# One core: an attention stage gives up the expert slots hidden in it, and the merge stage after it works all 128, sixteen to a tile

## The chip, the cores and the metric

The kernel runs on one core of one Trainium2 chip. The metric is the device time of one execution in microseconds. The compute engines named below are TensorE (PE; its weight loads are PEld), VectorE (DVE), ScalarE (ACT) and GpSimd (POOL); SyncE (SP) issues most transfers, and POOL issues the indirect ones, called gathers here.

## The reference, cut to what matters

Two groups of tokens, a sample of 256 and a prompt of 1024, pass through the same layer with the same weights: a mixer (a windowed attention A, a dense attention B, and a gated merge of the two), then a retrieval from 16384 experts, then a norm.

```python
def parallel_mixer(h, ...):
    ...
    oa = window_attention(...)
    ob = dense_attention(...)
    gates = sigmoid(h @ w_gate + b_gate); ga, gb = split(gates)
    merged = ga * (oa @ w_oa) + gb * (ob @ w_ob)
    return merged @ w_out

def peer(h, ...):                      # T tokens, 8 heads x 16 experts = 128 slots for each
    ...
    u, v = expert_u[idx], expert_v[idx]
    act = gelu(einsum('chkd,cd->chk', u, xc))
    return einsum('chk,chkd->cd', g * act, v)
```

For each token 128 experts are chosen. A slot is one expert for each of the 128 tokens of a tile: its rows (u and v, 2048 numbers for each token) are fetched from HBM, u is dotted with the token, the dot goes through gelu and is multiplied by the gate g, and v times that weight is added to a sum.

## The kernel before, in words

The program goes through stages with a barrier behind each (`build`): the sample's projection, attention, merge and choice of experts; then the prompt's projection, attention and merge, and last the prompt's experts. A stage works on tiles of 128 tokens, of which the sample has two and the prompt eight.

The choice of experts for the sample writes h, the indices and the gates g of both tiles to HBM, without fetching an expert. The fetching and summing for these two tiles is spread over the prompt's stages, beside their own work. Sample tile 0 runs in the prompt's projection (class `Background`). Sample tile 1 runs in the prompt's attention and merge (class `Hidden`, made by `Hiding(sample, 1)` in `build`). That second tile is what the change is about. Its parts are:

- `Hidden.load`: SP fetches h, the indices and g (line 260).
- `Hidden.gather_upto`: POOL issues one gather for a slot (line 283), 128 rows of 8 KB, into one of five ring places. From the sixth slot on it first waits until the slot five before it has been added.
- `Hidden.dot_of`: DVE multiplies u with h and sums (line 296); this waits for the gather to land.
- `Hidden.gelu`: ACT (line 334).
- `Hidden.add_of`: DVE forms the weight (line 305) and adds v times the weight to the sum (line 313). This frees the ring place.

In the attention stage (`phase_attend`) eight slots are worked in each of the eight prompt tiles, so 64 in all. A tile has eight steps g, one for each head of B and two of A, and `hide(i, 2g)` and `hide(i, 2g + 1)` place one dot or one add of the hidden tile into DVE's order, before and behind `max_b`. POOL computes the rotary embedding of the next tile and then issues the gathers. ACT evaluates four gelus at a time, at g = 1 and 5. When there is a hidden tile, two details differ: `Fills` gives all copies of transposed A probabilities (`pT_a`) to ACT, and ACT runs `exp_a` ahead of them. Without one, as in the sample's attention, ACT and DVE take one copy each and `exp_a` comes behind it.

In the merge stage (`phase_merge`) PE multiplies the mixed rows with `w_oa` and `w_ob` (four groups for a tile, line 1408), transposes the merged rows (line 1420), and multiplies with `w_out` (line 1431). DVE multiplies PE's results with the gates (`part`, line 1377, four for a tile), adds the two branches (`merged`, line 1383, two), and adds x (`xt`, line 1391, one). POOL adds the bias to the gates of a tile (`add_bias`, line 1322), and ACT takes the sigmoid (line 1350) and copies the transposed rows (line 1357). The function `turns` sets the order of the tiles: the branches of tile i are begun before the projection of tile i-1 is finished. The hidden work is spread by `Plan`: 2 x (128 - `first`) operations, one dot and one add for a slot, cut evenly over 48 places, of which a tile has six (two ahead of each half's products, as `hide(i, 0)` to `hide(i, 3)`, and two ahead of the `xt` of the tile before). With `first` = 64 a place holds 2 or 3 operations. `Plan.pool` lets POOL issue gathers up to five slots beyond what will have been added at that place, and POOL's order is written out: `add_bias(0)`, places 0 and 1, `add_bias(1)`, then in each tile three places, `add_bias(i + 1)`, three places.

`Early` fetches the first half of `w_oa` in the attention stage so that the merge has it at its start.

## Time and profile before

| what | value |
|---|---|
| median of the two runs | 4945.34 us (4940.06 to 4950.62) |
| the profiled execution's own time | 4939.81 us |
| its span, first to last instruction | 4937.9 us |
| busy in the span | PE 63%, DVE 68%, ACT 21%, POOL 35% |
| mean granted TensorE clock | 0.739 of full speed |
| moved by DMA | 1568.77 MB, mean 318 GB/s |

Times in the rows are microseconds from the start of the span unless marked ns. A row of the timeline gives the start, the duration, the engine, the line in the kernel, the operation with what it writes and reads, and in brackets how long the engine sat idle before it and who released it. A row that groups instructions gives the count, the busy time, the mean duration in ns and, behind the bar, the idle time of the engine in front of them. A row of the table by stretches gives the length of the stretch, then for each engine its busy time and number of instructions, then the granted clock, the share of the DMA engines' time that was used, and the rate.

### The profile page before, as it was taken

To read this page: it belongs to the slowest core of one execution; us is meant where nothing else is said; L and a number is where in the kernel's file an instruction comes from. 1 tells how busy PE (TensorE), PEld (TensorE's weight loads), DVE (VectorE), ACT (ScalarE), POOL (GpSimd) and SP (SyncE) were. 2 spreads that over 40 slices of the span, in tenths; PEclk is the share of its full clock that TensorE was granted. 3 is DMA by queue.
4 is the path that set the end of the run, shared out by engine and by line. 5 is a ranking of instruction groups with operands and counts; after the bars stand their busy time and mean duration, and the time that the engine had idled before them with its cause. 6 is when DMAs were issued, how large, how long until landed. Compare 5 with 4: busy or idle time off the path is not lost.

```text
span 4937.9 us, 72225 instructions
## 1 busy us (share of the span) xinstructions
PE 3098.5 (63%) x27052; PEld 1782.3 (36%) x27052; DVE 3340.8 (68%) x7744; ACT 1042.4 (21%) x2853; POOL 1728.8 (35%) x1393
## 2 busy tenths in 40 slices
PE   7686389885999989955545455445455444454433
PEld 6545367663777744432212112122122122121000
DVE  4426777786888866658867767667667577677554
ACT  3311111221555521111121121111211211211111
POOL 0200033323344323224444444444444444444443
PEclk9897699987999999966656666666566566565555
DMA  6143288897445477689999999999999999999998
GB/s 238 62 165 113 95 325 330 330 341 283 165 150 190 156 310 280 245 315 385 389 401 393 393 404 394 389 404 403 406 389 389 402 392 392 394 391 383 407 392 326
DMA packets 281852, 1568.77 MB, mean 318 GB/s; under 512 B 28064, under 2 KB 48032, under 8 KB 112928
## 3 DMA queue, kind: packets, MB, share of 16 engines
q0 software_dynamic: 184320, 1342.26, 68.9%
q1 hardware_dynamic: 97184, 221.90, 12.1%
q8 instruction: 215, 3.52, 0.3%
q14 instruction: 133, 1.09, 0.1%
HBM read 1510.52 MB, written 53.53 MB: 317 GB/s over the span
## 4 chain that ended last, share of the span: by engine, by line
DMA 32%; issue 7%; PE 7%; DVE 5%; POOL 4%; ACT 2%; another core or an unknown queue 0%; POOLq 0%; DVEq 0%; SPq 0%; ACTq 0%
DMA prompt_exp_ring<-in_experts_dram,prompt_exp_idx 29%; PE prompt_exp_acc L1966 6%; POOL prompt_exp_ring L1619 4%; DVE prompt_exp_junk L1864 3%; DMA prompt_exp_ring<-in_experts_dram,prompt_exp_idx_all 3%; ACT prompt_exp_diag L1696 2%; PE prompt_exp_qp L1927 1%; DVE prompt_exp_pos L1743 0%; DVE prompt_exp_best L1739 0%; PE prompt_exp_qp L1987 0%; DVE prompt_exp_dot L1864 0%; DMA prompt_exp_wq<-in_w_query_dram 0%; DVE prompt_exp_crest L1748 0%; DVE prompt_exp_topi L1743 0%
## 5 line engine op out<-in xcount | busy, mean ns | idle before, releaser
L1966 PE MATMUL prompt_exp_acc<-prompt_exp_ring,prompt_exp_diag 32*32 32x512 f32 x16384 | 936.3, 940 | 1396.1 <-ACT prompt_exp_diag L1696 1395.3
L1864 DVE CUSTOM_DVE_ANT_0 prompt_exp_junk<-prompt_exp_ring,prompt_exp_h_now 128x1024 bf16<-128x1024 f32 x1024 | 1244.9, 1227 | 698.3 <-DMA prompt_exp_ring<-in_experts_dram,prompt_exp_idx 654.0
L1619 POOL DMA_INDIRECT prompt_exp_ring<-in_experts_dram,prompt_exp_idx x896 | 1032.0, 1152 | 1369.8 <-PE prompt_exp_acc L1966 1205.3
L1966 PEld LDWEIGHTS prompt_exp_acc<-prompt_exp_ring,prompt_exp_diag 32*32 32x32 f32 x16384 | 168.6, 127 | 1948.6 <-issue 1945.9
L1690 ACT ACTIVATE prompt_exp_ge<-prompt_exp_dot 128x2 f32<-128x2 f32 x512 | 104.1, 203 | 2286.8 <-DVE prompt_exp_dot L1864 2286.6
L144 POOL DMA_INDIRECT bg_ring<-in_experts_dram,bg_idx x128 | 175.1, 1368 | 667.2 <-DVE bg_acc L180 367.3
L1927 PEld LDWEIGHTS prompt_exp_qp<-prompt_exp_hT,prompt_exp_wq 128*128 128x128 f32 x2048 | 314.6, 243 | 144.7 <-issue 141.8
L1927 PE MATMUL prompt_exp_qp<-prompt_exp_hT,prompt_exp_wq 128*128 128x128 f32 x2048 | 338.1, 334 | 4.2 <-DMA prompt_exp_wq<-in_w_query_dram 2.4
L283 POOL DMA_INDIRECT sample_hid_ring<-in_experts_dram,sample_hid_idx x128 | 131.8, 1030 | 512.7 <-DVE sample_hid_acc L313 496.0
L703 PE MATMUL prompt_proj_acc<-prompt_proj_w_hi,prompt_proj_hT_hi 128*128 128x512 f32 x640 | 261.1, 408 | 27.0 <-ACT prompt_proj_w_hi L596 23.1
L1696 ACT ACTIVATE prompt_exp_diag<-prompt_exp_fold,prompt_exp_wgt 128x32 f32<-128x32 f32 x1024 | 264.4, 306 | 0.4 <-issue 0.2
L704 PE MATMUL prompt_proj_acc<-prompt_proj_w_hi,prompt_proj_hT_lo 128*128 128x512 f32 x640 | 258.7, 404 | 0.0
L1619 POOL DMA_INDIRECT prompt_exp_ring<-in_experts_dram,prompt_exp_idx_all x128 | 150.7, 1178 | 267.7 <-PE prompt_exp_acc L1966 154.6
L169 DVE CUSTOM_DVE_ANT_0 bg_junk<-bg_ring,bg_h 128x1024 bf16<-128x1024 f32 x128 | 154.2, 1222 | 98.3 <-DMA bg_ring<-in_experts_dram,bg_idx 97.6
L296 DVE CUSTOM_DVE_ANT_0 sample_hid_junk<-sample_hid_ring,sample_hid_h 128x1024 bf16<-128x1024 f32 x128 | 202.1, 1579 | 20.3 <-DMA sample_hid_ring<-in_experts_dram,sample_hid_idx 10.8
L718 PE MATMUL prompt_proj_acc<-prompt_proj_w_lo,prompt_proj_hT_hi 128*128 128x512 f32 x640 | 172.0, 418 | 53.5 <-DVE prompt_proj_w_lo L639 53.5
L180 DVE SCALAR_TENSOR_TENSOR bg_acc<-bg_ring,bg_w,bg_acc 128x1024 f32<-128x1024 f32 x128 | 164.4, 1285 | 4.6
L313 DVE SCALAR_TENSOR_TENSOR sample_hid_acc<-sample_hid_ring,sample_hid_w,sample_hid_acc 128x1024 f32<-128x1024 f32 x127 | 163.0, 1283 | 2.9
L718 PEld LDWEIGHTS prompt_proj_acc<-prompt_proj_w_lo,prompt_proj_hT_hi 128*128 128x128 f32 x640 | 127.9, 202 | 88.6 <-DVE prompt_proj_w_lo L639 57.4
L1858 DVE TENSOR_TENSOR prompt_exp_wgt<-prompt_exp_ge,prompt_exp_g_now 128x2 f32<-128x2 f32 x512 | 83.0, 162 | 109.7 <-ACT prompt_exp_ge L1690 101.6
L703 PEld LDWEIGHTS prompt_proj_acc<-prompt_proj_w_hi,prompt_proj_hT_hi 128*128 128x128 f32 x640 | 124.2, 194 | 60.3 <-ACT prompt_proj_w_hi L596 25.6
L704 PEld LDWEIGHTS prompt_proj_acc<-prompt_proj_w_hi,prompt_proj_hT_lo 128*128 128x128 f32 x640 | 124.2, 194 | 29.9
(349 smaller groups left out, 5046.0 us busy)
## 6 DMA issues: line engine op xcount, KB each, us to landing
sample_proj_w<-in_w_all_dram SPq DMA_DIRECT2D x10, 2048.0 KB, 9.5
prompt_proj_w<-in_w_all_dram SPq DMA_DIRECT2D x10, 2048.0 KB
proj_dram<-prompt_proj_stage SPq DMA_DIRECT2D x80, 256.0 KB
prompt_exp_ring<-in_experts_dram,prompt_exp_idx POOLq DMA_INDIRECT x896
sample_exp_wq<-in_w_query_dram SPq DMA_DIRECT2D x4, 2048.0 KB, 15.5
prompt_att_q<-proj_dram SPq DMA_DIRECT2D x16, 512.0 KB
mixed_dram<-prompt_att_OT SPq DMA_DIRECT2D x8, 1024.0 KB, 3.8
prompt_mrg_mixT<-mixed_dram SPq DMA_DIRECT2D x8, 1024.0 KB
```

What stands on the lines that cost most here:

```text
L144: self.nc.gpsimd.indirect_dma_start(out=self.ring[:, k % self.RING, :], out_offset=None, in_=self.experts, in_offset=bass.IndirectOffsetOn ...
L180: last = nc.vector.scalar_tensor_tensor(self.acc[:], self.ring[:, (k + c) % self.RING, D:], self.w[:, c:c + 1], self.acc[:], ALU.mult, ALU ...
L296: self.nc.vector.tensor_tensor_reduce(out=self.junk[:], in0=self.ring[:, s % self.RING, 0:D], in1=self.h[:], scale=1.0, scalar=0.0, op0=AL ...
L313: nc.vector.scalar_tensor_tensor(self.acc[:], v, w, self.acc[:], ALU.mult, ALU.add).then_inc(self.added, 1)
L703: nc.tensor.matmul(acc[:, u % 4, :], hT_hi[:, k, cols], hi[:, k, :], start=(first and k == 0), stop=False)
L704: ins = nc.tensor.matmul(acc[:, u % 4, :], hT_lo[:, k, cols], hi[:, k, :], start=False, stop=(last and k == KD - 1))
L718: ins = nc.tensor.matmul(acc[:, u % 4, :], hT_hi[:, k, cols], lo[:, k, :], start=(first and k == 0), stop=(last and k == KD - 1))
L1619: nc.gpsimd.indirect_dma_start(out=ring[:, s % RING, :], out_offset=None, in_=experts, in_offset=bass.IndirectOffsetOnAxis(ap=column(s), a ...
L1696: last = nc.scalar.activation(diag[:, (g - 1) % 2, c, :], fold[:], ACT.Copy, scale=wgt[:, s:s + 1])
L1864: nc.vector.tensor_tensor_reduce(out=junk[:, s % 2, :], in0=ring[:, s % RING, 0:D], in1=h_now[:], scale=1.0, scalar=0.0, op0=ALU.mult, op1 ...
L1927: last = nc.tensor.matmul(qp[:, h % 2, p * P:(p + 1) * P], wq[:, k, (2 * h + p) * P:(2 * h + p + 1) * P], hT[:, k * P:(k + 1) * P], start= ...
L1966: last = nc.tensor.matmul(acc[at:at + Q, rows, :], diag[k, (g - 1) % 2, c, :], ring[k, s % RING, D + half * 512:D + half * 512 + 512], sta ...
```

## The change

`attend` for the prompt gets no hidden tile, and `merge` starts it at slot 0 instead of slot 64. The hidden tile's h, indices and gates are therefore loaded at the start of the merge, behind the first mixed rows and ahead of the weights.

```diff
@@ phase_merge, block.sync @@
                 load_mix(0)
                 if not bg:
                     early.load(sp)
+                elif first == 0:
+                    bg.load(sp)
                 for h in range(2):
@@ build @@
             early = Early(nc, Mem(nc, front, sems, "early"), w_oa)
-            attend(prompt, hidden, 0, early)
-            merge(prompt, hidden, SLOTS // 2, early)
+            attend(prompt, None, 0, early)
+            merge(prompt, hidden, 0, early)
         release(nc, sems)
```

The changed kernel's lines behind 1282 have numbers that are two higher. `Plan` now has 256 operations for the same 48 places, 5 or 6 in each. Three places of the program show what that does.

DVE in the merge, from the `xt` of one tile (line 1391, 1393 in the changed kernel) to the first `part` of the tile after the next (line 1377, 1379). Before:

```order
L1391 TENSOR_TENSOR prompt_mrg_xt<-prompt_mrg_Z,prompt_mrg_xt 128x1024
L305 TENSOR_TENSOR sample_hid_w<-sample_hid_ge,sample_hid_g 128x1
L313 SCALAR_TENSOR_TENSOR sample_hid_acc<-sample_hid_ring,sample_hid_w,sample_hid_acc 128x1024
L296 ISA sample_hid_junk,sample_hid_dot<-sample_hid_ring,sample_hid_h 128x1024
L296 ISA sample_hid_dot 128x1
L305 TENSOR_TENSOR sample_hid_w<-sample_hid_ge,sample_hid_g 128x1
L313 SCALAR_TENSOR_TENSOR sample_hid_acc<-sample_hid_ring,sample_hid_w,sample_hid_acc 128x1024
L1377 TENSOR_TENSOR prompt_mrg_part<-prompt_mrg_Y,prompt_mrg_gate 128x512
```

The same stretch in the changed kernel:

```order
L1393 TENSOR_TENSOR prompt_mrg_xt<-prompt_mrg_Z,prompt_mrg_xt 128x1024
L296 ISA sample_hid_junk,sample_hid_dot<-sample_hid_ring,sample_hid_h 128x1024
L296 ISA sample_hid_dot 128x1
L305 TENSOR_TENSOR sample_hid_w<-sample_hid_ge,sample_hid_g 128x1
L313 SCALAR_TENSOR_TENSOR sample_hid_acc<-sample_hid_ring,sample_hid_w,sample_hid_acc 128x1024
L296 ISA sample_hid_junk,sample_hid_dot<-sample_hid_ring,sample_hid_h 128x1024
L296 ISA sample_hid_dot 128x1
L305 TENSOR_TENSOR sample_hid_w<-sample_hid_ge,sample_hid_g 128x1
L313 SCALAR_TENSOR_TENSOR sample_hid_acc<-sample_hid_ring,sample_hid_w,sample_hid_acc 128x1024
L296 ISA sample_hid_junk,sample_hid_dot<-sample_hid_ring,sample_hid_h 128x1024
L296 ISA sample_hid_dot 128x1
L1379 TENSOR_TENSOR prompt_mrg_part<-prompt_mrg_Y,prompt_mrg_gate 128x512
```

A place held three hidden operations here (add, dot, add) and now holds five (dot, add, dot, add, dot).

POOL at the start of the merge. Before, with the gathers of the last attention tile in the first row (16 of them: eight of that tile and eight that go with the tile before):

```order
L283 DMA sample_hid_ring<-in_experts_dram,sample_hid_idx 128x2048 x16
L1322 TENSOR_TENSOR prompt_mrg_gate<-prompt_mrg_gate,prompt_mrg_bias 128x2048
L283 DMA sample_hid_ring<-in_experts_dram,sample_hid_idx 128x2048 x2
L1322 TENSOR_TENSOR prompt_mrg_gate<-prompt_mrg_gate,prompt_mrg_bias 128x2048
L283 DMA sample_hid_ring<-in_experts_dram,sample_hid_idx 128x2048 x6
L1322 TENSOR_TENSOR prompt_mrg_gate<-prompt_mrg_gate,prompt_mrg_bias 128x2048
L283 DMA sample_hid_ring<-in_experts_dram,sample_hid_idx 128x2048 x8
```

And in the changed kernel:

```order
L283 DMA sample_hid_ring<-in_experts_dram,sample_hid_idx 128x2048 x5
L1324 TENSOR_TENSOR prompt_mrg_gate<-prompt_mrg_gate,prompt_mrg_bias 128x2048
L283 DMA sample_hid_ring<-in_experts_dram,sample_hid_idx 128x2048 x4
L1324 TENSOR_TENSOR prompt_mrg_gate<-prompt_mrg_gate,prompt_mrg_bias 128x2048
L283 DMA sample_hid_ring<-in_experts_dram,sample_hid_idx 128x2048 x14
L1324 TENSOR_TENSOR prompt_mrg_gate<-prompt_mrg_gate,prompt_mrg_bias 128x2048
L283 DMA sample_hid_ring<-in_experts_dram,sample_hid_idx 128x2048 x16
```

The ring's first five gathers now stand in the merge ahead of the first `add_bias`, and nine of the 128 stand ahead of the second one, where 71 did.

ACT in the attention, one step with a transposed query (`qT`) between two others. Before:

```order
L1000 ACTIVATE prompt_att_prob_b,prompt_att_rsum<-prompt_att_Sb,prompt_att_nm 128x1024
L908 COPY prompt_att_qT<-prompt_att_tb 128x512
L334 ACT_TABLE_LOAD
L334 ACTIVATE sample_hid_ge<-sample_hid_dot 128x4
L908 COPY prompt_att_pT_b<-prompt_att_tb 128x512
L994 ACT_TABLE_LOAD
L994 ACTIVATE prompt_att_prob_a,prompt_att_rsum<-prompt_att_Sm,prompt_att_nm 128x385 x2
L908 COPY prompt_att_pT_a<-prompt_att_tb 128x384 x2
```

And in the changed kernel:

```order
L1000 ACTIVATE prompt_att_prob_b,prompt_att_rsum<-prompt_att_Sb,prompt_att_nm 128x1024
L908 COPY prompt_att_qT<-prompt_att_tb 128x512
L908 COPY prompt_att_pT_b<-prompt_att_tb 128x512
L908 COPY prompt_att_pT_a<-prompt_att_tb 128x384
L994 ACTIVATE prompt_att_prob_a,prompt_att_rsum<-prompt_att_Sm,prompt_att_nm 128x385 x2
```

The gelu and two loads of a function table are gone from ACT; it copies one `pT_a` of a step instead of two (DVE does the other) and computes the exponentials of A behind it.

## Rows read from the trace of the kernel before

**Rows 1.** The page, the chain that ended last, by line.

```profile
DMA prompt_exp_ring<-in_experts_dram,prompt_exp_idx 29%; PE prompt_exp_acc L1966 6%; POOL prompt_exp_ring L1619 4%; DVE prompt_exp_junk L1864 3%; DMA prompt_exp_ring<-in_experts_dram,prompt_exp_idx_all 3%; ACT prompt_exp_diag L1696 2%; PE prompt_exp_qp L1927 1%; DVE prompt_exp_pos L1743 0%; DVE prompt_exp_best L1739 0%; PE prompt_exp_qp L1987 0%; DVE prompt_exp_dot L1864 0%; DMA prompt_exp_wq<-in_w_query_dram 0%; DVE prompt_exp_crest L1748 0%; DVE prompt_exp_topi L1743 0%
```

**Rows 2.** Stretches: the attention's tiles, the merge's start, one merge tile.

```profile
1262.00:1757.00 495.00, 462.08 (x3182) 358.58 (x3179) 428.18 (x922) 284.93 (x602) 190.04 (x120) 1.00 0.44 162
1757.00:1800.00 43.00, 32.44 (x69) 14.23 (x70) 15.89 (x23) 5.38 (x8) 9.01 (x4) 0.81 0.92 361
1966.80:2008.80 42.00, 42.00 (x105) 19.07 (x104) 26.66 (x39) 7.11 (x12) 13.25 (x9) 1.00 0.72 275
```

**Rows 3.** Timeline of DVE in the merge, late.

```profile
1954.41 1.22 DVE L296 CUSTOM_DVE_ANT_0 sample_hid_junk<-sample_hid_ring,sample_hid_h 128x1024 bf16<-128x1024 f32 x1
...
1956.95 1.22 DVE L296 CUSTOM_DVE_ANT_0 sample_hid_junk<-sample_hid_ring,sample_hid_h 128x1024 bf16<-128x1024 f32 x1
...
1966.76 1.23 DVE L1391 TENSOR_TENSOR prompt_mrg_xt<-prompt_mrg_Z,prompt_mrg_xt 128x1024 f32<-128x1024 f32 x1 [6.04 <-PE prompt_mrg_Z L1431]
...
2008.84 1.23 DVE L1391 TENSOR_TENSOR prompt_mrg_xt<-prompt_mrg_Z,prompt_mrg_xt 128x1024 f32<-128x1024 f32 x1 [6.05 <-PE prompt_mrg_Z L1431]
```

**Rows 4.** Groups of DVE in the merge, 1757 to 2110.

```profile
L1377 DVE TENSOR_TENSOR prompt_mrg_part<-prompt_mrg_Y,prompt_mrg_gate 128x512 f32<-128x512 f32 x32 | 22.1, 690 | 71.2 <-PE prompt_mrg_Y L1408 52.2 <-ACT prompt_mrg_gate L1350 19.1
L1383 DVE TENSOR_TENSOR prompt_mrg_merged<-prompt_mrg_part 128x512 f32<-128x512 f32 x16 | 14.7, 917 | 1.9 <-PE prompt_mrg_tb L1420 1.5
```

**Rows 5.** Timeline of POOL and DVE, one of two `add_bias` and its neighbour.

```profile
1863.28 5.11 POOL L1322 TENSOR_TENSOR prompt_mrg_gate<-prompt_mrg_gate,prompt_mrg_bias 128x2048 f32<-128x2048 f32 x1 [3.98 <-DMA prompt_mrg_gate<-proj_dram]
1863.94 5.53 DVE L296 CUSTOM_DVE_ANT_0 sample_hid_junk<-sample_hid_ring,sample_hid_h 128x1024 bf16<-128x1024 f32 x1
...
1985.55 4.52 POOL L1322 TENSOR_TENSOR prompt_mrg_gate<-prompt_mrg_gate,prompt_mrg_bias 128x2048 f32<-128x2048 f32 x1
...
1988.78 1.31 DVE L305 TENSOR_TENSOR sample_hid_w<-sample_hid_ge,sample_hid_g 128x1 f32<-128x1 f32 x1
```

**Rows 6.** Timeline of SP, PE, POOL and DVE, the merge's start.

```profile
1762.75 0.32 SPq L1272 DMA_DIRECT2D prompt_mrg_mixT<-mixed_dram  x1
1767.56 10.19 PE L1408 MATMUL prompt_mrg_Y<-early_w,prompt_mrg_mixT 128*128 128x512 f32 x16 [14.61 <-DMA prompt_mrg_mixT<-mixed_dram]
1777.99 4.50 POOL L1322 TENSOR_TENSOR prompt_mrg_gate<-prompt_mrg_gate,prompt_mrg_bias 128x2048 f32<-128x2048 f32 x1 [26.62 <-DMA prompt_mrg_bias<-in_b_gate_dram]
1784.46 0.69 DVE L1377 TENSOR_TENSOR prompt_mrg_part<-prompt_mrg_Y,prompt_mrg_gate 128x512 f32<-128x512 f32 x1 [19.05 <-ACT prompt_mrg_gate L1350]
1797.96 4.50 POOL L1322 TENSOR_TENSOR prompt_mrg_gate<-prompt_mrg_gate,prompt_mrg_bias 128x2048 f32<-128x2048 f32 x1 [5.82 <-DMA prompt_mrg_gate<-proj_dram]
```

**Rows 7.** The tile `prompt_mrg_xt`: its DVE instructions, first and last start.

```profile
L1391 DVE TENSOR_TENSOR prompt_mrg_xt<-prompt_mrg_Z,prompt_mrg_xt x8: 1224/1224/1226, 1840.5 to 2109.0; 128x1024 f32<-128x1024 f32 x8
```

**Rows 8.** The tile `sample_hid_ring`: landing of gathers, issued 1800 to 1850, then to 2093.

```profile
DMA to landing us min/median/max: 8.2/12.3/16.5
...
DMA to landing us min/median/max: 5.6/6.1/11.3
```

**Rows 9.** Stretch in the prompt's experts.

```profile
3000.00:4000.00 1000.00, 491.28 (x6852) 200.88 (x6852) 685.40 (x1773) 155.71 (x624) 431.95 (x376) 0.63 0.99 397
```

**Rows 10.** DMA queues in the merge, 1757 to 2110: packets, MB, share.

```profile
q0 software_dynamic: 8517, 61.96, 45.7%
q1 hardware_dynamic: 9338, 38.29, 27.6%
```

**Rows 11.** Waits of PE in the attention, 1262 to 1757: us, times, longest.

```profile
PE prompt_att_tb L1134 <- ACT prompt_att_prob_b L1000: 11.8, 12, 1.1
PE prompt_att_Op L1194 <- ACT prompt_att_pT_a L908: 9.7, 14, 0.7
PE prompt_att_tb L1134 <- ACT prompt_att_OT L908: 5.0, 6, 0.8
```

**Rows 12.** Timeline of DVE and PE, the attention's first tile.

```profile
1221.04 6.00 DVE L296 CUSTOM_DVE_ANT_0 sample_hid_junk<-sample_hid_ring,sample_hid_h 128x1024 bf16<-128x1024 f32 x1 [2.62 <-DMA sample_hid_ring<-in_experts_dram,sample_hid_idx]
1229.67 1.97 PE L1134 MATMUL prompt_att_tb<-prompt_att_ident,prompt_att_prob_b 128*128 128x128 f32 x8 [5.70 <-ACT prompt_att_prob_b L1000]
```

## The prediction

> **What bounds the kernel now.** I read the chain that ended last, then the table by stretches, then the timeline of each engine in the merge. The chain is mostly the gathers of the prompt's experts [rows 1]. That stage comes behind a barrier, holds none of the changed work, and should keep its length. So the question is the length of two stages ahead of it.
>
> In the attention's tiles PE is busy 462 of 495 us, DVE 428 [rows 2]. The end is PE's, with some waits. The last merge tiles are PE alone: 42.0 of 42.0 us, DVE only 26.7 [rows 2], and DVE sits 6 us in front of `xt` waiting for PE [rows 3]. Two `xt` are 42.08 us apart [rows 3]: that is a merge tile now. The merge runs from SP's first load at 1762.75 [rows 6], which I call M, to the last `xt`, which starts at 2109.0 and takes 1.2 [rows 7]: M + 347.5.
>
> **What the attention gains.** It loses 64 slots, that is 64 dots, 64 adds, 16 weight products, 16 gelus with two table loads each, the loads of h, indices and gates, and 69 gathers. What of that is on PE's path is what PE waited for. Between 1262 and 1757 it waited 11.8 us for `prob_b` and 5.0 us for the copy of `OT` [rows 11]. Both come late because hidden dots stand in front of `max_b` on DVE, so I count both as gone: 17. The 9.7 us put down to `pT_a` [rows 11] fall where PE waits for DVE's division, in front of which nothing hidden stands; they stay. In the first tile one hidden dot takes 6.00 us and PE then waits 5.70 [rows 12], its next matmuls running slower; I take 8 for this. One `pT_a` copy of a step moves to DVE, behind `max_b`: DVE has lost two hidden operations of about 1.2 us in that step, and PE has 16 products of B in between, so it costs nothing. ACT now has `exp_a` behind that copy; losing one copy covers it. If that cover failed it would be some 0.5 us for each of 64 steps, 32. I take -25, with bounds -36 (all waits gone) and +7 (cover failed).
>
> **What the merge's DVE must do.** Two dots with one weight product and one add between them start 1954.41 and 1956.95, so a slot costs 2.54 [rows 3]. Sixteen are 40.6. The tile's own products by mean duration are 4 x 0.69 + 2 x 0.92 [rows 4] + 1.2 for `xt` [rows 7] = 5.8. Consecutive operations overlap by some 7% (a slot's durations add up to more than its spacing), so 5.4. Together 46.0 against PE's 42.08. DVE takes PE's place as the bound, even if nothing else happens.
>
> Something else does: `add_bias`. POOL's operation ran 1863.28 to 1868.39, and a dot that DVE started at 1863.94 took 5.53 instead of 1.22; in a later tile the one-column weight product, started inside POOL's 4.52 us, ended when POOL did [rows 5]. (The Trainium skill, GPSIMD Engine Reference, Specifications, says that POOL's SBUF interfaces are shared with VectorE, with contention for instructions with two SBUF inputs. Dot, weight product and add are such; by this rule every `add_bias` stops DVE's now unbroken row of them, by its absence a tile would be 46.) Now DVE was mostly waiting for PE meanwhile; with DVE busy throughout, each costs up to 4.5. A tile: 50.5.
>
> **What the DMA must do.** Experts are fetched at 376 gathers in 1000 us with the engines at 0.99 [rows 9]: 2.66 for a slot of 1.05 MB. Sixteen are 42.6; a tile also moves 3.15 MB (mixed rows, gates, x in, x2 out), 7.7 at about 410 GB/s: 50.3. DVE and DMA would both be nearly full, with a ring of five between them. A gather in the loaded part of the merge takes 12.3 us to land, in the unloaded part 6.1 [rows 8]. A ring place is held for the wake and issue on POOL (0.8), the landing, and two dots and two adds with weights (5.1): five slots in 12.0 or 18.2 us, 2.4 or 3.6 for one. The tile allows 50.5/16 = 3.15. So it is sometimes short. Also, while `add_bias` runs, POOL issues nothing and the DMA engines run dry. I take 53.5 for the first six tiles and 51 for the last two, which load no more mixed rows or gates: mean 53. The bounds are 46.0 (no stop, no wait) and 16 x 3.6 = 58.
>
> **The start of the merge.** Before, the ring was full and DVE's first `part` started at M + 21.7, behind a bias that landed at M + 15.2; the second `add_bias` had its gates at M + 35.2 [rows 6]. Now h (0.6 MB with indices and gates) goes ahead of the weights, and POOL issues five gathers (5.2 MB) before its first `add_bias`. At the 361 to 410 GB/s seen [rows 2], with the two queues sharing, the bias lands near M + 24 and the first `part` starts at about M + 30. Only nine gathers stand ahead of the second `add_bias`. Its gates lie behind 12 MB of direct loads, and 9.4 MB of gathers join them: M + 54. DVE uses up its nine slots by about M + 49 and waits: `add_bias` to M + 58.5, issue, a landing of 8 to 10: M + 68. By then 17 of the 256 hidden operations are done.
>
> **The sum.** 239 operations are left, 32 to a tile: 7.47 tiles x 53 = 396. M + 68 + 396 = M + 464; the last projection on PE is longer than the two places beside it by some 3, and `xt` is 1.2: M + 468. Against M + 347.5 that is +120. With the attention's -25: +95. The profiled execution is 4939.8, its span 1.9 less; that gives 5035. The median shown is 5.5 above it, so I say 5038.
>
> **Rivals.**
> (a) The stops of `add_bias` fall mostly into waits that exist anyway and the ring keeps up: a tile is 47 to 48. 68 + 7.47 x 47.5 + 4 = 427: +79 - 25 = +54, 4997. For it: DVE paid only about 1.2 for such a stop late in the merge [rows 5]. Against it: then DVE was idle half of the time.
> (b) The ring decides: 58 for a tile. 68 + 433 + 4 = 505: +158 - 25 = +133, 5075. For it: the landing of 12.3 when loaded [rows 8]. Against it: DMA is at 0.72 in a present tile [rows 2] and a landing there is 6.1.
> (c) HBM limits lower, at the 361 GB/s of the merge's start [rows 2] for as long as both queues are full. Then 38.3 MB [rows 10] and 134 MB of gathers take 477, the end is M + 485: +138 - 25 = +113, 5056. Against it: the experts run at 397 [rows 9] for a thousand microseconds. (The Trainium skill, DMA: Bandwidth & Descriptors, Where 436 GB/s comes from, names about 358 GB/s as what binds between HBM and SBUF on a core, and by it the merge would take 481; the trace's 397 disagrees.)
> (d) Not slower: DVE takes the eight further slots into its waits. It decides if a tile's DVE work stays below 46 with the start as before. Then M + 21.7 + 7.85 x 46 + 4 = M + 387: +39, and with the attention's full -36 it is +3, 4945; with a `part` that overlaps better, some us below before. For it: DVE idles 15.4 of 42 [rows 2]. Against it: eight slots are 20.3, more than 15.4, and the ring is empty at the start.
> (e) That the change does less than it says can't be: the orders show all 128 slots in the merge.
>
> **How the numbers follow.** Forecast 0.52, own range 5010 to 5065. (a) 0.21, (b) 0.19, (c) 0.03, (d) 0.05. The range 4980 to 5085 leaves out most of (d) and the far end of (b). Slower by over 2%, which is about what a measurement of this kernel can tell from no change, begins at 5044: all of (b) and (c) and two fifths of the forecast, 0.43. Within 2%: 0.56. Faster by over 2%: 0.01, since not even all of the attention's waits together with the smallest merge give 99 us.
>
> **What would show it.** Right: attention tiles some 2 us shorter (the `OT` stores closer together), no PE wait for `prob_b` of more than a few us in sum; in the merge two `xt` 50 to 56 us apart, PE with idle time in front of the branches waiting for DVE's `part`, DVE over 85% busy, a dot or weight product of some 5 us beside nearly every `add_bias`; a first `part` near M + 30; a DVE wait for a gather of over 10 us near M + 50; DMA share above 0.9. Wrong: `xt` 42 us apart with DVE waiting for PE (then (d)), or over 57 with DVE waiting for the ring after most slots (then (b)), or an attention that isn't shorter.

## The result and the profile after

The changed kernel takes 5046.3 us (two runs, 5039.9 and 5052.8) against 4945.3 of the kernel before: ratio 1.0208, interval 1.0189 to 1.0228. It is slower by 101 us, and the interval lies on both sides of 2%. The forecast was 5038, its own range 5010 to 5065.

The page of the changed kernel, its span, busy times, DMA and chain:

```profile
span 5038.0 us, 72280 instructions
PE 3111.4 (62%) x27052; PEld 1781.5 (35%) x27052; DVE 3348.6 (66%) x7856; ACT 980.5 (19%) x2805; POOL 1742.5 (35%) x1393
...
DMA packets 281852, 1568.77 MB, mean 311 GB/s; under 512 B 28064, under 2 KB 48032, under 8 KB 112928
...
DMA 31%; issue 7%; PE 7%; DVE 6%; POOL 4%; ACT 2%; POOLq 0%; DVEq 0%; SPq 0%; ACTq 0%
```

The chain still ends in the experts' gathers, as in [rows 1]. It does not tell where 100 us came from: followed back, it begins at 2217.4 us, with the first loads of the experts' stage, and the two stages that changed lie ahead of the barrier before that. So they are measured by their marks: SP's first load of each and the last `xt`.

| | before | after |
|---|---|---|
| attention, first load to the merge's first load (M) | 573.9 | 542.7 |
| M in the trace | 1762.75 | 1728.70 |
| first `xt` | M + 77.8 | M + 129.1 |
| end of the last `xt` | M + 347.5 | M + 477.6 |
| one full merge tile | 42.08 | 55.96 |
| from there to the end of the span | 2827.7 | 2831.7 |

Attention -31.2, merge +130.1, an attention that starts 2.8 earlier, 4.0 behind the merge: +100 of span. The last two are within what the other runs show: the attention starts between 1186.0 and 1193.4 in them, and for the stage behind the merge see below.

**The attention.** The stretch of its tiles and the groups of PE in it (busy, mean ns | idle before, releaser), changed kernel:

```profile
core 0: us, PE busy (x) PEld busy (x) DVE busy (x) ACT busy (x) POOL busy (x), PEclk, DMA share, GB/s
1262.00:1720.00 458.00, 447.93 (x3103) 350.28 (x3103) 271.30 (x769) 210.19 (x485) 111.75 (x60) 1.00 0.11 38
```

```profile
L1194 PE MATMUL prompt_att_Op<-prompt_att_vB,prompt_att_pT_b 128*128 128x128 f32 x928 | 114.1, 276 | 9.7 <-DVE prompt_att_O L1061 9.7
...
L1134 PE MATMUL prompt_att_tb<-prompt_att_ident,prompt_att_prob_b 128*128 128x128 f32 x464 | 63.3, 279 | 0.0
```

These answer to [rows 2] and [rows 11]: the waits for `prob_b` and `OT` are gone, and the 9.7 that [rows 11] puts down to `pT_a` stay, now named `prompt_att_O`, which is DVE's division.

**The merge's start.** POOL and DVE, changed kernel (start, us, ... [idle before <-releaser]); this answers to [rows 6]:

```profile
1750.44 4.49 POOL L1324 TENSOR_TENSOR prompt_mrg_gate<-prompt_mrg_gate,prompt_mrg_bias 128x2048 f32<-128x2048 f32 x1 [8.31 <-DMA prompt_mrg_bias<-in_b_gate_dram]
...
1785.61 4.51 POOL L1324 TENSOR_TENSOR prompt_mrg_gate<-prompt_mrg_gate,prompt_mrg_bias 128x2048 f32<-128x2048 f32 x1 [16.29 <-DMA prompt_mrg_gate<-proj_dram]
```

```profile
1746.18 1.23 DVE L296 CUSTOM_DVE_ANT_0 sample_hid_junk<-sample_hid_ring,sample_hid_h 128x1024 bf16<-128x1024 f32 x1 [17.35 <-DMA sample_hid_ring<-in_experts_dram,sample_hid_idx]
1750.92 5.10 DVE L296 CUSTOM_DVE_ANT_0 sample_hid_junk<-sample_hid_ring,sample_hid_h 128x1024 bf16<-128x1024 f32 x1 [3.50 <-DMA sample_hid_ring<-in_experts_dram,sample_hid_idx]
...
1799.99 1.22 DVE L296 CUSTOM_DVE_ANT_0 sample_hid_junk<-sample_hid_ring,sample_hid_h 128x1024 bf16<-128x1024 f32 x1 [16.79 <-DMA sample_hid_ring<-in_experts_dram,sample_hid_idx]
```

With an empty ring DVE's first dot waits 17.4 us. Behind the second `add_bias`, which waits 16.3 for tile 1's gates with the gathers queued behind it, DVE waits 16.8, and dots again at M + 71.3.

**A merge tile.** The last `xt` group, then stretches: a long one, and two microseconds at a time around one `add_bias`, which POOL ran 2002.42 to 2007.35 with a dot of 5.53 us beside it:

```profile
L1393 DVE TENSOR_TENSOR prompt_mrg_xt<-prompt_mrg_Z,prompt_mrg_xt x8: 1216/1217/1225, 1857.8 to 2205.1; 128x1024 f32<-128x1024 f32 x8
```

```profile
core 0: us, PE busy (x) PEld busy (x) DVE busy (x) ACT busy (x) POOL busy (x), PEclk, DMA share, GB/s
1860.00:2080.00 220.00, 175.53 (x411) 78.15 (x410) 196.15 (x282) 31.09 (x77) 99.23 (x67) 0.89 0.91 356
...
1992.00:1996.00 4.00, 4.00 (x6) 1.44 (x6) 2.59 (x4) 0.20 (x1) 2.28 (x2) 0.51 1.01 426
...
2004.00:2006.00 2.00, 2.00 (x6) 0.90 (x5) 2.00 (x1) 0.00 (x0) 2.00 (x1) 1.00 0.96 397
2006.00:2008.00 2.00, 2.00 (x6) 0.81 (x5) 2.00 (x1) 0.00 (x0) 1.85 (x2) 1.00 0.16 66
2008.00:2010.00 2.00, 2.00 (x6) 0.95 (x5) 1.97 (x5) 0.20 (x1) 1.26 (x1) 1.00 0.08 12
2010.00:2012.00 2.00, 2.00 (x6) 0.89 (x5) 1.97 (x4) 0.20 (x1) 1.14 (x1) 1.00 0.93 279
```

Groups of DVE and PE from 1860 to 2080, and below them the same stretch in the kernel before:

```profile
L296 DVE CUSTOM_DVE_ANT_0 sample_hid_junk<-sample_hid_ring,sample_hid_h 128x1024 bf16<-128x1024 f32 x64 | 95.4, 1490 | 21.1 <-DMA sample_hid_ring<-in_experts_dram,sample_hid_idx 20.9
L1379 DVE TENSOR_TENSOR prompt_mrg_part<-prompt_mrg_Y,prompt_mrg_gate 128x512 f32<-128x512 f32 x16 | 11.0, 686 | 0.0
...
L1433 PE MATMUL prompt_mrg_Z<-prompt_mrg_wo,prompt_mrg_mT 128*128 128x512 f32 x128 | 65.0, 673 | 44.5 <-ACT prompt_mrg_mT L1359 44.5
```

```profile
1860.00:2080.00 220.00, 220.00 (x544) 99.67 (x543) 141.91 (x204) 35.76 (x61) 69.97 (x47) 1.00 0.70 266
```

Read them together. DVE is busy 196.2 of 220, that is 49.9 of a tile of 55.96, and waits for nothing of PE (0.0 before `part`); it waits 20.9 us for gathered rows, 5.3 a tile. PE, which had 220 busy of 220, now waits 44.5 for `mT`, a copy of what DVE merged. The two engines have changed roles. And the stop does two things at once: DVE stands still, so it frees no place, and POOL issues nothing, so the queued gathers land and the DMA engines fall from 397 to 66 and 12 GB/s.

**Where in the tile the rows come late.** One tile of the changed kernel in order of time, up to 1920: SP's three loads for the next tile, every wait of DVE for a row, and `add_bias`:

```profile
1866.28 0.33 SPq L1278 DMA_DIRECT2D prompt_mrg_xt<-in_x_dram  x1
1866.66 0.57 SPq L1272 DMA_DIRECT2D prompt_mrg_mixT<-mixed_dram  x1
1867.28 0.46 SPq L1275 DMA_DIRECT2D prompt_mrg_gate<-proj_dram  x1
1870.81 1.22 DVE L296 CUSTOM_DVE_ANT_0 sample_hid_junk<-sample_hid_ring,sample_hid_h 128x1024 bf16<-128x1024 f32 x1 [1.03 <-DMA sample_hid_ring<-in_experts_dram,sample_hid_idx]
1874.37 1.23 DVE L296 CUSTOM_DVE_ANT_0 sample_hid_junk<-sample_hid_ring,sample_hid_h 128x1024 bf16<-128x1024 f32 x1 [0.93 <-DMA sample_hid_ring<-in_experts_dram,sample_hid_idx]
1879.19 1.23 DVE L296 CUSTOM_DVE_ANT_0 sample_hid_junk<-sample_hid_ring,sample_hid_h 128x1024 bf16<-128x1024 f32 x1 [0.74 <-DMA sample_hid_ring<-in_experts_dram,sample_hid_idx]
1884.15 1.23 DVE L296 CUSTOM_DVE_ANT_0 sample_hid_junk<-sample_hid_ring,sample_hid_h 128x1024 bf16<-128x1024 f32 x1 [2.34 <-DMA sample_hid_ring<-in_experts_dram,sample_hid_idx]
1889.35 4.93 POOL L1324 TENSOR_TENSOR prompt_mrg_gate<-prompt_mrg_gate,prompt_mrg_bias 128x2048 f32<-128x2048 f32 x1
1917.99 1.23 DVE L296 CUSTOM_DVE_ANT_0 sample_hid_junk<-sample_hid_ring,sample_hid_h 128x1024 bf16<-128x1024 f32 x1 [0.68 <-DMA sample_hid_ring<-in_experts_dram,sample_hid_idx]
```

The other three tiles of the stretch look alike: 18.8 of the 20.9 us lie within 20 us behind SP's loads of the next tile's x, mixed rows and gates, and none within 16 us behind an `add_bias`. Gathers issued between 1870 and 1880 took a median of 12.6 us to land, those between 1894 and 1914, behind the addition, 6.7. So it is the tile loads that make rows late. The dry time behind the stop, when DVE stands still as well, does not.

### The profile page after: what moved, and what is told of

Same layout as the page of the kernel before. It is cut to its first block, busy times and chain, and to the rows that moved or that the text cites. A ratio compares the mean times of both kernels' runs of the same rounds, so it can differ in the third digit from the quotient of the medians.

```text
span 5038.0 us, 72280 instructions
## 1 busy us (share of the span) xinstructions
PE 3111.4 (62%) x27052; PEld 1781.5 (35%) x27052; DVE 3348.6 (66%) x7856; ACT 980.5 (19%) x2805; POOL 1742.5 (35%) x1393
## 4 chain that ended last, share of the span: by engine, by line
DMA 31%; issue 7%; PE 7%; DVE 6%; POOL 4%; ACT 2%; POOLq 0%; DVEq 0%; SPq 0%; ACTq 0%
DMA prompt_exp_ring<-in_experts_dram,prompt_exp_idx 28%; PE prompt_exp_acc L1968 6%; POOL prompt_exp_ring L1621 4%; DVE prompt_exp_junk L1866 3%; DMA prompt_exp_ring<-in_experts_dram,prompt_exp_idx_all 3%; ACT prompt_exp_diag L1698 2%; PE prompt_exp_qp L1929 1%; DVE prompt_exp_pos L1745 0%; DVE prompt_exp_best L1741 0%; DVE prompt_exp_dot L1866 0%; DMA prompt_exp_wq<-in_w_query_dram 0%; DVE prompt_exp_hit L1788 0%; DVE prompt_exp_hit L1782 0%; DVE prompt_exp_crest L1750 0%; DVE prompt_exp_sel L1792 0%
## 5 line engine op out<-in xcount | busy, mean ns | idle before, releaser
L144 POOL DMA_INDIRECT bg_ring<-in_experts_dram,bg_idx x128 | 178.3, 1393 | 660.0 <-DVE bg_acc L180 360.4
L283 POOL DMA_INDIRECT sample_hid_ring<-in_experts_dram,sample_hid_idx x128 | 156.8, 1225 | 364.3 <-DVE sample_hid_acc L313 223.8
L296 DVE CUSTOM_DVE_ANT_0 sample_hid_junk<-sample_hid_ring,sample_hid_h 128x1024 bf16<-128x1024 f32 x128 | 186.0, 1453 | 74.2 <-DMA sample_hid_ring<-in_experts_dram,sample_hid_idx 74.0
L1433 PE MATMUL prompt_mrg_Z<-prompt_mrg_wo,prompt_mrg_mT 128*128 128x512 f32 x256 | 127.0, 659 | 82.5 <-ACT prompt_mrg_mT L1359 67.6
L718 PEld LDWEIGHTS prompt_proj_acc<-prompt_proj_w_lo,prompt_proj_hT_hi 128*128 128x128 f32 x640 | 130.1, 205 | 86.0 <-DVE prompt_proj_w_lo L639 54.2
## 6 DMA issues: line engine op xcount, KB each, us to landing
sample_exp_wq<-in_w_query_dram SPq DMA_DIRECT2D x4, 2048.0 KB, 18.2
```

The lines of the kernel that those rows point to most:

```text
L144: self.nc.gpsimd.indirect_dma_start(out=self.ring[:, k % self.RING, :], out_offset=None, in_=self.experts, in_offset=bass.IndirectOffsetOn ...
L296: self.nc.vector.tensor_tensor_reduce(out=self.junk[:], in0=self.ring[:, s % self.RING, 0:D], in1=self.h[:], scale=1.0, scalar=0.0, op0=AL ...
L718: ins = nc.tensor.matmul(acc[:, u % 4, :], hT_hi[:, k, cols], lo[:, k, :], start=(first and k == 0), stop=(last and k == KD - 1))
```

## Experiments

My theory for the tile was a sum: DVE's work 45.9, the stop 4.3, rows that come late 5 to 6. The rivals: DMA is the floor and everything on DVE is only its shadow; or PE's chain holds all. Repeats set the scale: 19 runs of the kernel before, taken together, lay between 4935.6 and 4957.9, two single ones beside other experiments came to 4954.2 and 4930.3, and the stage behind the merge took 2812 to 2838 in the runs of the table, though nothing in it differs. A single total says little below 20 us, so what follows rests on marks inside each trace: "tile" is a fifth of the time from the first `xt` to the sixth, "end" the end of the last `xt` after M. The total is that of the traced execution, for e11 and e12 the median of ten (their traced ones took 4942.6 and 4952.9).

| run | tile | first `xt` | end | total |
|---|---|---|---|---|
| before | 42.08 | M + 77.8 | M + 347.5 | 4939.8 |
| changed | 55.96 | M + 129.1 | M + 477.6 | 5039.9 |
| e1 half the slots | 42.09 | M + 96.0 | M + 365.7 | 4924.9 |
| e2 no bias addition | 51.89 | M + 124.6 | M + 454.1 | 5000.9 |
| e3 half the rows | 52.20 | M + 120.9 | M + 446.3 | 5005.8 |
| e4 no sum | 51.99 | M + 123.6 | M + 447.0 | 4999.6 |
| e5 half the rows, no bias | 47.87 | M + 111.6 | M + 415.7 | 4975.5 |
| e6 bias on VectorE | 53.93 | M + 127.0 | M + 466.9 | 5032.9 |
| e7 ring filled early | 56.25 | M + 114.9 | M + 464.9 | 5013.1 |
| e8 second bias late | 55.85 | M + 126.1 | M + 474.4 | 5032.7 |
| e9 ring of seven | 50.31 | M + 125.0 | M + 442.0 | 5010.2 |
| e10 no sum, no bias | 48.82 | M + 121.5 | M + 430.3 | 4988.3 |
| e11 four a tile, 96 in the merge | 45.21 | M + 96.3 | M + 378.9 | 4948.3 |
| e12 the same, bias on VectorE | 45.82 | M + 94.7 | M + 379.2 | 4945.2 |

**e1: the attention's gain and the start alone.**

```diff
-        plan = Plan(first, SLOTS - first, PLACES * G, 1, 1)
+        plan = Plan(first, SLOTS // 2 if bg else SLOTS, PLACES * G, 1, 1)
```

> The changed kernel with only 64 of the second sample tile's 128 slots worked at all, eight to a tile of the merge, none in the attention; the other 64 are left out of the computation. It holds the attention's gain and the merge's new start alone. My theory (the loss is the 16 slots a tile, the start adds some 20 us): attention 542.7 us as in the changed kernel (573.9 before), tiles of the merge back at TensorE's 42.1 us, merge end at M+365 to M+375 (M+347.5 before), total about 4933 us. Rival (the start alone costs most of the +130, by the weights that come late): merge end beyond M+420, total above 4985. Rival (the attention's gain is given back behind it): attention again near 570.

The attention took 542.4 again, the tile fell back to 42.09, the end came at M + 365.7. In the groups of the trace DVE waits for PE again before `xt`:

```profile
L1393 DVE TENSOR_TENSOR prompt_mrg_xt<-prompt_mrg_Z,prompt_mrg_xt x8: 1223/1225/1226, 1831.0 to 2099.4; 128x1024 f32<-128x1024 f32 x8
its engine sat idle before it (us, times) until:
  PE prompt_mrg_Z L1433: 45.3, 8
```

So the new start, with an empty ring and the loads of h ahead of the weights, costs 18.2 of the 130; the attention's gain is real and is not given back; the other 112 are the eight further slots to a tile.

**e2 to e5: take a load off each side.** e2 leaves out `add_bias` on POOL, e3 every second gather, e4 the sum, e5 is e2 and e3 in one.

```diff
 def add_bias(i):
     pool.wait_ge(gate_ld[i % 2], 16 * (i // 2 + 1))
+    if bg:
+        pool.sem_inc(biased, 1)
+        return
...
-            nc.vector.scalar_tensor_tensor(self.acc[:], v, w, self.acc[:], ALU.mult, ALU.add)
+            nc.vector.tensor_scalar(self.acc[:, 0:1], v[:, 0:1], w, None, ALU.mult)
...
+            if not (s < self.RING or s % 2 == 0):
+                continue
             self.nc.gpsimd.indirect_dma_start(
```

> The changed kernel, the prompt's merge without GpSimd's addition of the gates' bias; the bias is left out of the computation there. A: VectorE's stop of 4.3 us beside that addition is a real term of the tile and the waits for gathers (5.0) stay: tiles of 51 to 52 us instead of 56.0, merge end near M+448, total near 5015. B: DMA decides and the stop only overlaps with it, the time comes back as waits for gathers: tiles of 55 to 56, total 5035 to 5046.

> The changed kernel with every second gather of an expert row left out after the first five slots; VectorE works all 128 slots with the same instructions, every second one on the row that lies in the ring already. A and B: the waits for gathers (5.0 us a tile) go, VectorE's 45.9 and its stop of 4.3 stay: tiles of 50.2 us, merge end near M+440, total near 5008. Rival (waits for gathers hide a VectorE that would be late anyway, by PE or ACT): tiles stay above 54. Also asked: does the start (first dot at M+17.5, VectorE out of work from M+53 to M+71) get shorter, as DMA is less full? If it is the ring of five slots behind the second bias addition's gate load, the stop stays about 16 us.

> The changed kernel where each slot's addition (1024 columns into the sum) is cut to a product of one column; the sum over the slots is left out. VectorE's work a tile falls from 45.9 to about 31 us, all gathers stay. A (the tile is VectorE's work plus stops plus late rows, and DMA has room): tiles fall to TensorE's 42 to 45 us, total near 4965. B (DMA is a floor by itself: 19.9 MB a tile at 397 GB/s are 50.3 us): tiles of 50 to 52 us, merge end near M+435, total near 5005.

> The changed kernel with both edits of the earlier runs: every second gather left out after the first five slots, and the bias addition of the prompt's merge left out of the computation. Alone, they brought the tile from 56.0 to 52.2 and 51.9 us. Theory D (two near floors: VectorE with its work of 45.9 and the stop of 4.3, and DMA with 19.9 MB at 392 GB/s, 50.8, and 4 to 5 us in which it runs dry behind the stop): with both the tile is VectorE's work alone, 46 to 47 us, merge end near M+415, total near 4975. Rival (something common to all three, TensorE's lowered clock or the chain Y, gate, merged, transpose, Z, holds the tile at 52): tiles of 51 to 52, total above 4998.

The stretch 1860 to 2080 of e2 (columns as in the stretches above):

```profile
1860.00:2080.00 220.00, 185.97 (x443) 82.78 (x441) 193.38 (x301) 35.46 (x86) 83.70 (x69) 0.94 0.98 387
```

The dots' group of e2 in it:

```profile
L296 DVE CUSTOM_DVE_ANT_0 sample_hid_junk<-sample_hid_ring,sample_hid_h 128x1024 bf16<-128x1024 f32 x68 | 83.0, 1221 | 23.7 <-DMA sample_hid_ring<-in_experts_dram,sample_hid_idx 23.4
```

The same stretch of e3, and then its dots:

```profile
1860.00:2080.00 220.00, 181.52 (x425) 80.58 (x423) 207.08 (x301) 35.71 (x85) 59.84 (x38) 0.92 0.62 230
```

```profile
L301 DVE CUSTOM_DVE_ANT_0 sample_hid_junk<-sample_hid_ring,sample_hid_h 128x1024 bf16<-128x1024 f32 x68 | 100.1, 1473 | 10.0 <-DMA sample_hid_ring<-in_experts_dram,sample_hid_idx 10.0
```

The same stretch of e4, and then its dots:

```profile
1860.00:2080.00 220.00, 186.89 (x440) 82.87 (x438) 141.71 (x302) 35.78 (x86) 85.23 (x73) 0.94 0.95 385
```

```profile
L296 DVE CUSTOM_DVE_ANT_0 sample_hid_junk<-sample_hid_ring,sample_hid_h 128x1024 bf16<-128x1024 f32 x69 | 103.3, 1496 | 76.0 <-DMA sample_hid_ring<-in_experts_dram,sample_hid_idx 75.9 <-issue 0.2
```

e2: the dots fell from 1490 ns to 1221, so the stop sat in them and comes from POOL's addition; the tile fell by 4.1, about the stop. The waits for rows stayed at 5.5 a tile (23.4 in 220 us of 51.9 each). Case A held for the tile; the end came 6 us later than I had put it. e3: DVE busy 49.1 of 52.2, waits for rows down to 2.4 a tile, DMA at 0.62. Its tile is 2 above what was expected, since those waits did not vanish. e4: DVE is busy 33.5 of the tile instead of 49.9, and the tile fell by only 4.0, with dots waiting 18 us a tile for rows. That is case B: with DVE this light, DMA decides. DVE's load and DMA's are both near the tile, and neither is a shadow of the other. e5, with both loads lower, came to 47.87 and M + 415.7 where 46 to 47 and M + 415 stood: the rival of something common at 52 is out.

The start in e3: DVE still waited 17.3 us for its first row, but behind the second `add_bias` only 8.0 instead of 16.8. With half the gathers gone, tile 1's gates landed 5 us earlier after M (that `add_bias` started at M + 52.0 for M + 56.9). My expectation there, 16 us, missed.

**e10: DMA alone.** e4 with e2's edit.

> The changed kernel without the sum over the slots (one column instead of 1024) and without the prompt's bias addition, both left out of the computation; all gathers and loads stay. VectorE's work is some 31 us a tile and GpSimd only issues gathers, so what is left is DMA alone beside TensorE's 42.1. If the 52.0 us of the run without the additions were 19.9 MB at the 420 GB/s of its undisturbed stretches plus 4 us dry behind the stop: tiles of 47.5 to 49. If DMA alone takes 50.8 (392 GB/s): tiles of 50 to 51. If DMA is no floor below this: 42.1 to 45.

```profile
1860.00:2080.00 220.00, 199.02 (x469) 88.48 (x468) 130.04 (x317) 36.82 (x88) 71.26 (x71) 0.95 1.01 410
```

Here the DMA engines are full throughout, at 410 GB/s, and a tile of 19.9 MB took 48.82: DMA's own floor. e4 took 3.2 more with the same gathers; that is what the dry time behind a stop costs DMA.

**e9: a deeper ring.**

```diff
-    RING = 5
+    RING = 7
...
-        wo = m.sb("wo", [P, KD, D])
+        wo = m.sb("wo", [P, KD, 512 if bg else D])
```

> The changed kernel with a ring of seven gathered rows instead of five. To make room, only the first half of w_out is held in the merge and used for both halves of Z (the second half of w_out is left out of the computation; TensorE does the same work), and the ring is allocated after the attention. E: the some 5 us a tile by which the tile of 56.0 exceeds each engine's own sum (VectorE 50.2, DMA 50.8) come from a ring too short to bridge the stop and the tile loads, where two near floors alternate: tiles of 51 to 53 us. Rival (DMA's dry time behind the stop is lost whatever the depth, and tile loads take their share): tiles stay at 55 to 56.

```profile
1860.00:2080.00 220.00, 188.81 (x437) 83.74 (x436) 215.89 (x313) 36.72 (x87) 102.73 (x75) 0.92 0.99 398
```

```profile
L296 DVE CUSTOM_DVE_ANT_0 sample_hid_junk<-sample_hid_ring,sample_hid_h 128x1024 bf16<-128x1024 f32 x71 | 90.5, 1274 | 1.0 <-DMA sample_hid_ring<-in_experts_dram,sample_hid_idx 1.0
```

This settles the 5.3 us. With two more places the waits for rows fell from 20.9 to 1.0 in 220 us, DVE was busy 98%, and the tile was 50.31: DVE's sum of 50.2 and nothing else. `add_bias` still ran on POOL and still stopped DVE, only more often in a weight product than in a dot. What two more places bought is that tile loads no longer made rows late; the DMA engines, at 0.99, did not run dry behind the stop either, but in the changed kernel that had cost DVE no wait (above). e2, without a stop, fits: it waited 5.5, again behind the tile loads, and of those 2.9 are DMA's floor (48.8 by e10) above DVE's 45.9. e9 is no usable kernel: the room for the two places came from half of `w_out`.

**e6: the bias on VectorE.**

```diff
+                        if bg and h == 1 and br == 0 and i + 1 < G:
+                            add_bias(i + 1)
```

> The changed kernel with the merge's bias addition done by VectorE instead of GpSimd (same sum, nothing left out): no VectorE dot lies beside a GpSimd addition any more, VectorE gets 2.4 us more a tile (two of its 1.22 us additions of 1024 columns). Theory D: VectorE 48.3, DMA 50.8 and never dry: tiles of 51 to 52.5 us, first tile some 5 us later as VectorE waits for the bias (M+22), total near 5005. Rival (the addition costs on either engine the same, since gathers are freed late by it): tiles of 54 to 56, total above 5020.

VectorE added 2048 columns in 2.28 us where POOL takes 4.5 and stops VectorE for 4.3. The dots were back at 1221 ns, and the tile was 53.93, of which DVE is busy 47.9 (195.4 in 220) and waits 5.3 for rows (21.6 in 220). I had expected DMA's floor with nothing on top, and that missed: the tile lies between my two cases, and the total of 5032.9 where only the rival had it. The gain of 2.0 a tile is what DVE saved, and the waits for rows did not move.

**e7 and e8: the start.** e7 issues the hidden tile's loads and first gathers in the attention; e8 moves one call.

```diff
                 gather(0, 0, 1)
-                add_bias(1)
                 gather(0, 2, 3)
+                add_bias(1)
```

> The changed kernel with the hidden tile's three loads and its first five gathers moved from the merge's start into the attention (loads at tile 4, gathers at tile 6 of 8). Theory (part of the start's cost is the empty ring and SP's loads ahead of the weights): first dot at M+1 to M+3 instead of M+17.5, first xt at M+112 to M+120 instead of M+129, total 10 to 17 us less than the changed kernel, near 5032. Rival (the weights, bias and gates land as late as before and VectorE has nothing to do behind its first slots): less than 5 us.

> The changed kernel with GpSimd's second bias addition, of tile 1, put behind the gathers of places 2 and 3 instead of ahead of them. Theory (GpSimd waits for tile 1's gate with the gathers queued behind it, so VectorE runs out of rows for 16.8 us, M+54 to M+71): the stop goes, first xt 8 to 16 us earlier, total near 5034. Rival (DMA is full with weights and gates then, rows would be as late): less than 4 us; or the later addition makes VectorE wait for tile 1's sigmoid by as much as was won.

e7: first `xt` 14.2 earlier, end 12.7 earlier, within the range, and an attention of 542.5 in spite of five gathers in it. (The total fell by 26.8; most of the rest lies in the unchanged stage behind the merge, 2812.5 here.) The first dot started at M + 0.2. Then DVE waited 20.6 us for a gelu that on ACT stands behind tile 0's sigmoid, which waits for the bias: the empty ring was not the only thing in front of the first slots. e8: 3.0 earlier, the rival's size. The single wait of 16.8 is gone, and many of 0.5 to 2.7 us stand in its place: rows came late one by one, with the DMA engines full either way.

**e11 and e12: between the two kernels.** Four slots to a tile in the attention, all in its second half, and twelve to a tile in the merge; e12 with the bias of tiles 2 to 7 on VectorE.

```diff
-        PER = 8
+        PER = 4
...
+                    if place < 8:
+                        return
+                    four, stage, n = 0, place // 4 % 2, place % 4
...
-            merge(prompt, hidden, SLOTS // 2, early)
+            merge(prompt, hidden, SLOTS // 4, early)
```

> The kernel before with four slots to a tile of the attention instead of eight (32 in all, in the second half of each tile) and 96 in the merge, twelve to a tile; nothing left out. Attention: half of the gain of 31.2 us, 558 us. Merge tile by single sums: TensorE 42.1, VectorE 12 x 2.54 + 5.4 + 4.3 = 40.2, DMA 15.7 MB at 392 GB/s = 40. If a tile is the largest of them: 42.1, merge end M+350 to M+358, total 4930 to 4940, some 8 us under the kernel before. If near floors lose some us where they alternate, as the changed kernel's tile does: tiles of 44 to 46, total 4945 to 4965, no gain or a loss.

> The same with the bias of tiles 2 to 7 added by VectorE (2.3 us) instead of GpSimd (VectorE's stop of 4.3 and DMA's dry time); nothing left out. If the stop is what makes the near floors lose time: tiles of 42.1 to 43, total 5 to 15 us under the run with four a tile. If not: within 3 us of it.

Ratios to the kernel before: e11 1.0008 (0.9998 to 1.0019), e12 0.9998 (0.9983 to 1.0014). Neither differs from it. In e11 the merge went as the second case says, a tile of 45.21. But the attention took 544.6, not 558. PE's groups from 1262 to 1720 in e11, and the dots of its merge:

```profile
L1196 PE MATMUL prompt_att_Op<-prompt_att_vB,prompt_att_pT_b 128*128 128x128 f32 x912 | 112.2, 276 | 9.7 <-ACT prompt_att_pT_a L908 9.7
...
L1136 PE MATMUL prompt_att_tb<-prompt_att_ident,prompt_att_prob_b 128*128 128x128 f32 x464 | 63.4, 280 | 0.0
```

```profile
L296 DVE CUSTOM_DVE_ANT_0 sample_hid_junk<-sample_hid_ring,sample_hid_h 128x1024 bf16<-128x1024 f32 x61 | 94.0, 1540 | 25.7 <-DMA sample_hid_ring<-in_experts_dram,sample_hid_idx 25.5
```

PE's waits are those of an attention without any slot, and the `OT` stores come 63.92 us apart in both, 67.30 in the kernel before. (The 3.4 us stand in five of the seven distances; the last two differ by 0.8 and 0.0.) So thirty-two slots add nothing to the tiles, and the other thirty-two cost all of the 3.4 us each. Whether that is their number or their place in the first half of a tile was not separated. Free of cost they are not quite: from the last `OT` store to M it took 7.75 us in e11 and 9.19 in e12, for 5.13 without slots. The merge gives it back: 45.21 is DVE's 39.7 and 5.2 of waits for rows (25.5 in 220), though TensorE alone would be 42.1, DVE's work lies below it and DMA is at 0.88. So e11's sum against the kernel before is: attention -29.3, merge +31.4.

In e12 the dots' waits fell to 9.3, but the addition itself waited, in DVE's order, for its gates to land:

```profile
L1376 DVE TENSOR_TENSOR prompt_mrg_gate<-prompt_mrg_gate,prompt_mrg_bias 128x2048 f32<-128x2048 f32 x5 | 11.5, 2292 | 27.4 <-DMA prompt_mrg_gate<-proj_dram 27.4
```

5.7 us a tile, more than was won. I had put it too early, so this run does not tell whether the stop is what near floors lose by.

## Why the prediction was right, and where only its sum was

**Attention, -25.** It was -31.2. The waits counted as gone went, those counted as staying stayed. By the `OT` stores, tiles 2 to 8 took 429.7 instead of 447.4: 17.7 for my 17. The first tile took 9.7 less for my 8. The 3.9 left are the gap from the last `OT` store to M, 8.99 before and 5.13 after: I had not looked at it. e11 and e12, with slots, show 7.75 and 9.19, so hidden work near the barrier lengthens it; by what was not tried. The `pT_a` copy that moved to DVE cost nothing: in e11 it is still ACT's, and the stores are as far apart.

**DVE's work, 46.0, and the stop, 4.5.** Right: 49.9 busy in the changed tile, 50.31 the whole tile in e9. The stop was 4.3 in nearly every tile, for dots that happened to start beside `add_bias`; e2 confirms the cause. (The Trainium skill, GPSIMD Engine Reference, Specifications, says that the two engines share SBUF interfaces and contend when VectorE's instruction has two SBUF inputs. The traces agree, and show a full stop, 5.53 us for 1.22.)

**DMA's 50.3.** It was 48.8 by e10. The rate was 410 GB/s, not 397. (c) falls by that: a rate of 361 was the merge's start and not a limit. (The Trainium skill, DMA: Bandwidth & Descriptors, Where 436 GB/s comes from, has about 358 GB/s as what binds between HBM and SBUF. The 410 over 220 us on this one core disagree. The Trainium skill, HBM Reference, Specifications (TRN2), takes 358 as a core's share with both of a pair streaming and about 425 for one alone. With that the trace agrees.)

**The tile, 53.5 for six and 51 for two.** This is the term that was mis-sized. It was 55.96, then 49.2 for the seventh. I had allowed 3 us for late rows. They were 5.3, and stayed at 5.2 to 5.5 in e2, e6 and e11, with DVE's work anywhere between 40 and 50 us a tile (in e2 partly as DMA's own floor). My way of sizing it, the mean landing of a gather against the time of five slots, was the wrong one: landings from 1860 to 2080 had a median of 8.2 us, which a ring of five allows. What decides is the worst stretch, the landings behind the tile loads, where the waits lie: 12.6 us in the median there, and 12.4 one tile later. I had also named the dry time of the DMA engines behind `add_bias` as a reason for late rows; no wait followed it within 16 us. e9 shows that places bridge the stretch: 1.0 us of waits with seven. The dry time has a price only where DMA is the bound (e4 against e10, 3.2 us a tile).

**The start.** Bias at M + 21.7 for M + 24, first `part` M + 33.1 for M + 30, second `add_bias` M + 56.9 for M + 54, DVE's first dot behind it M + 71.3 for M + 68. Each is within 3.3 us. By e1, of the 51.3 us by which the first `xt` is later, 18.2 are the start and the rest the tile's own further slots.

**One sign in the wrong place.** I had PE idle in front of the branches, waiting for DVE's `part`. It idles in front of `Z`, for `mT` (44.5 us in 220), and 0.0 before the branches.

**The sum, +95.** From M + 71.3, 7.47 tiles took 402 (53.8 each for my 53), and the end was M + 477.6 for M + 468. The merge came out 10 worse and the attention 6 better: -31.2 and +130.1 against -25 and +120. That the sum is nearer than its terms is luck. One addition was also wrong: 5035 and the 5.5 from the profiled execution to the median make 5040, and my 5038 took only half of the 5.5.

**The rivals.** (a) Stops hidden, 47 to 48: no, the stop is paid (e2 -4.1 a tile). (b) Ring decides, 58: no, since the tile follows DVE's work (e2, e5, e6); but its mechanism, a ring too short for slow landings, takes 5.3 of the tile. (d) Not slower: no. In e1, with eight slots to a tile of 42.09, DVE waits 14.4 us of it for PE, and eight further slots are 20.3.

## What to carry to other kernels

Two engines that are each nearly full do not give the larger of two sums. With a short ring between them they gave one engine's sum and a toll, some 5 us a tile here. Look at what shares the DMA engines with the gathers: here the toll lay behind the tile loads. Buy places before moving work, if there is room for them: two more took it to 0.2, but here cost half of a weight matrix.

An instruction that stops its neighbour also stops what the neighbour would have freed. Price it on every queue that lives from those places, but only if that queue is the bound: the DMA engines' dry time cost 3.2 us a tile where they were (e4), and nothing that the trace shows in the changed kernel.

Before moving all hidden work out of a stage, ask which part of it costs. Here half of it cost the tiles nothing, and nearly all of the price was in the other half.

## What was not expected of the hardware

The DMA engines ran at 410 GB/s for 220 us with no stop and little on DVE (e10), 398 with DVE full (e9).

TensorE's granted clock, 1.00 over the stretch 1860 to 2080 before, was 0.89 in the changed kernel: in each tile PE waited 9.2 to 14.4 us for `mT`, the clock fell while it did, and stood at 0.51 when it began to work again (1992 to 1996 above), the lower of its levels of 1.2 and 2.4 GHz. Then it came back to 1.00. Z's products took a mean of 673 ns, for 592 before. It cost nothing in this stretch, as DVE did not wait for PE in it; with PE back as the bound it may.

**Left open.** Where between four and eight slots an attention tile starts to pay, a merge with ten slots to a tile (e11 had twelve), and a version with seven places and the whole of w_out were not tried. No version run here beats the kernel before.
